# Gate projections in the context steps of two scans: four of 32 moved from the last output steps

## The reference

```python
def token_mixers(h, conv_fn, init_states, with_output, w_in, ...):
    (q_m, k_m, v_m, o_m, gate_m, q_g, k_g, v_g, r_g, lr_g, mg_m, mg_g) = jnp.split(h @ w_in, cuts, axis=-1)
    ...
    hm_f, st_mf = mlstm_scan(qm, km, vm, gm[0, 0], gm[0, 1], st_mf, with_output)
    hm_b, st_mb = mlstm_scan(flip_t(qm), flip_t(km), flip_t(vm), flip_t(gm[1, 0]), flip_t(gm[1, 1]), st_mb, with_output)
    ...
    og_f, st_gf = gla_scan(qg, kg, vg, split_heads(log_a[0], GLA_HEADS), st_gf, with_output)
    og_b, st_gb = gla_scan(flip_t(qg), flip_t(kg), flip_t(vg), flip_t(split_heads(log_a[1], GLA_HEADS)), st_gb, with_output)
    ...
    y_m = merge_heads_rms(hm_f + flip_t(hm_b), ml_norm, h.dtype) * jax.nn.sigmoid(o_m)
    y_g = merge_heads_rms(og_f + flip_t(og_b), gla_norm, h.dtype) * jax.nn.silu(r_g)
    y = jax.nn.sigmoid(mg_m) * (y_m @ w_proj_m) + jax.nn.sigmoid(mg_g) * (y_g @ w_proj_g)
```

## Time and profile before

| what | value |
|---|---|
| median of 3 runs | 2488.88 us (2486.9 to 2498.27) |
| profiled execution | 2488.79 us |
| its span, first to last instruction | 2487.1 us |
| TensorE, VectorE, ScalarE, GpSimd busy | 87%, 57%, 41%, 34% of the span |
| mean granted TensorE clock | 0.935 |
| mLSTM scan, first to last matmul | 641.2 to 955.0 us |
| GLA scan, first to last matmul | 961.5 to 1427 us |

### The profile page before, as it was taken

The page is one execution under the profiler, slowest core; times in us unless marked ns, Lnnn a source line. Parts: engine busy times, 40 slices in busy tenths (PEclk is TensorE's granted clock), DMA queues, the critical chain, the costliest instruction groups (busy, mean ns, idle before and its releaser), DMA issues. The chain is left out here.

```text
span 2487.1 us, 26742 instructions
## 1 busy us (share of the span) xinstructions
PE 2170.5 (87%) x10286; PEld 1756.2 (71%) x10286; DVE 1421.4 (57%) x1711; ACT 1009.6 (41%) x1263; POOL 846.4 (34%) x630
## 2 busy tenths in 40 slices
PE   6979979995599995799999959999759899999992
PEld 1268868884487884688888737788557778887882
DVE  0536542102433332788988535444258899998993
ACT  1422210111144443355455444432216676766762
POOL 5300000100255664366766511220112344443441
PEclk9989999997799997899999969999859999999996
DMA  7733324212354665233345376573348966459535
GB/s 275 247 75 97 98 85 170 80 51 109 120 181 150 177 182 179 80 128 119 115 124 136 77 227 208 159 228 115 106 185 342 360 223 192 118 178 344 154 60 161
DMA packets 262890, 398.75 MB, mean 160 GB/s; under 512 B 27046, under 2 KB 186918, under 8 KB 255980
## 3 DMA queue, kind: packets, MB, share of 16 engines
q1 hardware_dynamic: 233068, 243.90, 30.9%
q0 software_dynamic: 27968, 147.89, 19.0%
q10 hardware_dynamic: 1728, 5.25, 0.6%
HBM read 401.68 MB, written 88.67 MB: 197 GB/s over the span
## 5 line engine op out<-in xcount | busy, mean ns | idle before, releaser
L2584 DVE TENSOR_TENSOR ex_w_lo<-ex_raw,ex_w_hi 128x2048 fp32r<-128x2048 f32 x186 | 415.9, 2283 | 40.4 <-ACT ex_w_hi L2446 40.4
L2446 ACT ACTIVATE ex_w_hi<-ex_raw 128x2048 fp32r<-128x2048 f32 x182 | 337.8, 1909 | 177.6 <-DMA ex_raw<-in_w_up_dram,rt_w_rows 99.6
L682 POOL DMA_DIRECT2D vals<-rows_stage x40 | 21.8, 545 | 438.5 <-ACT rows_stage L674 438.5
L2316 POOL DMA_INDIRECT ex_raw<-in_w_up_dram,rt_w_rows x60 | 73.7, 1229 | 147.5 <-DVE ex_w_lo L2584 142.3
L2009 DVE TENSOR_TENSOR mo_w_lo<-mo_w,mo_w_hi 128x1024 fp32r<-128x1024 f32 x48 | 59.8, 1245 | 102.6 <-ACT mo_w_hi L1906 102.5
L1544 PEld LDWEIGHTS gl_lv_ps<-gl_q_level,gl_k_level 128*128 128x128 f32 x896 | 108.1, 194 | 11.0 <-issue 8.2
L2316 POOL DMA_INDIRECT ex_raw<-in_w_down_dram,rt_w_rows x30 | 52.4, 1748 | 183.2 <-DVE ex_w_lo L2584 183.2
L1544 PE MATMUL gl_lv_ps<-gl_q_level,gl_k_level 128*128 128x64 f32 x896 | 110.5, 276 | 3.3 <-DVE gl_scores L1674 1.7
L908 PE MATMUL gl_u_ps<-half_hi,gl_u_w_hi 128*128 128x512 f32 x256 | 108.0, 422 | 4.6 <-ACT gl_u_exp L926 4.6
L908 PE MATMUL ml_u_ps<-half_hi,ml_u_w_hi 128*128 128x512 f32 x256 | 105.4, 412 | 7.2 <-ACT ml_u_exp L926 7.2
L2120 PE MATMUL mo_ps<-mo_branch_hi,mo_w_hi 128*128 128x512 f32 x256 | 105.5, 412 | 6.9 <-DVE mo_w_lo L2009 6.4
(11 more groups left out here) (401 smaller groups left out, 6058.9 us busy)
## 6 DMA issues: line engine op xcount, KB each, us to landing
fr_w<-in_w_mod_dram SPq DMA_DIRECT2D x12, 2048.0 KB, 10.4
ml_u_w<-in_w_in_dram SPq DMA_DIRECT2D x32, 512.0 KB
gl_u_w<-in_w_in_dram SPq DMA_DIRECT2D x32, 512.0 KB, 5.0
vals<-rows_stage POOLq DMA_DIRECT2D x40, 256.0 KB, 2.3
ml_v<-vals SPq DMA_DIRECT2D x20, 512.0 KB, 3.9
gl_v<-vals SPq DMA_DIRECT2D x20, 512.0 KB, 3.4
qk_w<-in_w_in_dram SPq DMA_DIRECT2D x16, 512.0 KB, 4.8
rows_w<-in_w_in_dram SPq DMA_DIRECT2D x8, 1024.0 KB, 7.1
```

The lines of the kernel that those rows point to most:

```text
L2316: pool.indirect_dma_start(out=raw[:, q, :], out_offset=None, in_=sources[q], in_offset=bass.IndirectOffsetOnAxis(ap=w_rows[:, q, b:b + 1], ...
L2446: act.activation(hi[:, q, h], raw[:, q, h], ACT.Copy).then_inc(hi_done[q], 1)
L2584: dve.tensor_tensor(lo[:, q, at], raw[:, q, at], hi[:, q, at].bitcast(F32), ALU.subtract)\
```

## The change

The 32 units of each scan are given out in another way. Units 0 to 3 stand in the context steps 0 to 3, one each, behind the state products. Output steps 4 to 15 have two units each as before (`unit_in(u)` = 2n + 4 and `unit_after(u)` = 2n + 5), and output steps 16 to 19 have one each, units 28 to 31, in the first of the two places. In the mLSTM scan the transposes of the keys for steps 1 to 4 now stand ahead of the unit of the step before. The loads, the weight copies, the subtractions, `take`, `plus_one`, `finish` and the stores are given out in step with it on SyncE, ScalarE and GpSimd. The wait for the GLA scan's half of the tokens goes with its first unit to step 0. No instruction is added or removed in count.

```diff
@@ -853,6 +853,25 @@
     return 2 * i + 1 - u % 2
 
 
+ONE_UNIT = FIRST_OUT
+
+
+def unit_in(u):
+
+    n = u - FIRST_OUT
+    if n < 0:
+        return None
+    return FIRST_OUT + 2 * n - max(0, n - (OUTS - ONE_UNIT))
+
+
+def unit_after(u):
+
+    n = u - FIRST_OUT
+    if n < 0:
+        return u if u >= 0 else None
+    return unit_in(u) + 1 if n < OUTS - ONE_UNIT else None
+
+
 class GateUnits:
...
@@ -1030,22 +1049,21 @@
             load_rows(FIRST_OUT + 1)
             for u in range(STEPS):
                 n = u - FIRST_OUT
-                if n >= 0:
-                    units.load(sp, 2 * n + 2)
-                    units.load(sp, 2 * n + 3)
-                if n >= 1:
-                    units.store(sp, 2 * n - 2)
+                for g in (unit_in(u), unit_after(u)):
+                    if g is not None:
+                        units.load(sp, g + 2)
+                if unit_in(u - 1) is not None:
+                    units.store(sp, unit_in(u - 1))
                 if FIRST_OUT + 2 <= u + 2 < STEPS:
                     load_rows(u + 2)
-                if u + 2 < STEPS and n < 0:
+                if n < 0:
                     load_v(u + 2)
-                if n >= 1:
-                    units.store(sp, 2 * n - 1)
+                if unit_after(u - 1) is not None:
+                    units.store(sp, unit_after(u - 1))
                 if n >= 0 and first_visit(u):
                     store_h(u)
-                if u + 2 < STEPS and n >= 0:
+                if n >= 0 and u + 2 < STEPS:
                     load_v(u + 2)
-            units.store(sp, UNITS - 2)
             units.store(sp, UNITS - 1)
             units.all_stored(sp)
             for d in range(2):
@@ -1170,16 +1184,19 @@
                 n = u - FIRST_OUT
                 if n >= 0:
                     products(u)
-                if kept(u):
+                if kept(u) and not 0 < u <= FIRST_OUT:
                     keys(u)
                 if n >= 0:
-                    units.multiply(pe, 2 * n)
+                    units.multiply(pe, unit_in(u))
                     outputs(u)
                 if kept(u):
                     state(u, 0)
-                if n >= 0:
-                    units.multiply(pe, 2 * n + 1)
-                if kept(u):
+                if n < 0:
+                    state(u, 1)
+                    keys(u + 1)
+                if unit_after(u) is not None:
+                    units.multiply(pe, unit_after(u))
+                if kept(u) and n >= 0:
                     state(u, 1)
 
         @block.vector
...
@@ -1408,23 +1427,21 @@
             units.low(pool, 0)
             units.low(pool, 1)
             for u in range(STEPS):
-                n = u - FIRST_OUT
+                n, g, late = u - FIRST_OUT, unit_in(u), unit_after(u - 1)
                 if n >= 0:
                     inter(u)
-                if n >= 1:
-                    units.plus_one(pool, 2 * n - 1)
-                    units.scale(pool, 2 * n - 2)
-                    units.low(pool, 2 * n + 1)
-                    if not first_visit(u - 1):
-                        add_o(u - 1)
+                if late is not None:
+                    units.plus_one(pool, late)
+                    units.scale(pool, late - 1)
+                    units.low(pool, late + 2)
+                if n >= 1 and not first_visit(u - 1):
+                    add_o(u - 1)
                 if FIRST_OUT <= u + 1 < STEPS:
                     lower_levels(u + 1)
-                if n >= 0:
-                    units.plus_one(pool, 2 * n)
-                    if n >= 1:
-                        units.scale(pool, 2 * n - 1)
-                    units.low(pool, 2 * n + 2)
-            units.plus_one(pool, UNITS - 1)
+                if g is not None:
+                    units.plus_one(pool, g)
+                    units.scale(pool, g - 1)
+                    units.low(pool, g + 2)
             add_o(STEPS - 1)
 
         @block.scalar
@@ -1480,27 +1497,29 @@
             units.high(act, 0)
             units.high(act, 1)
             for u in range(STEPS):
-                n = u - FIRST_OUT
+                n, g, late = u - FIRST_OUT, unit_in(u), unit_after(u - 1)
+                if n >= 0 and late is not None:
+                    units.take(act, late)
                 if n >= 1:
-                    units.take(act, 2 * n - 1)
                     leave(u - 1)
                 if kept(u):
                     keys_out(u)
-                if n >= 1:
-                    units.high(act, 2 * n + 1)
-                    units.finish(act, 2 * n - 2)
+                if n >= 0 and late is not None:
+                    units.high(act, late + 2)
+                    units.finish(act, late - 1)
                 if u + 1 < STEPS:
                     logs(u + 1)
-                if n >= 0:
-                    units.take(act, 2 * n)
-                    units.high(act, 2 * n + 2)
-                if n >= 1:
-                    units.finish(act, 2 * n - 1)
+                if n < 0 and late is not None:
+                    units.take(act, late)
+                    units.high(act, late + 2)
+                    units.finish(act, late - 1)
+                if g is not None:
+                    units.take(act, g)
+                    units.high(act, g + 2)
+                    units.finish(act, g - 1)
                 if u + 1 < STEPS:
                     factors(u + 1)
-            units.take(act, UNITS - 1)
             leave(STEPS - 1)
@@ -1576,25 +1595,29 @@
                 if n < 0:
                     decays(u + 1)
                     state_sum(u)
+                    if u == 0:
+                        pe.wait_ge(half_loaded, 32)
+                    units.multiply(pe, unit_after(u))
                 else:
+                    g, late = unit_in(u), unit_after(u)
                     level(u, 0)
                     if u + 1 < STEPS:
                         decays(u + 1)
                     level(u, 1)
                     diagonal(u)
-                    if n == 0:
-                        pe.wait_ge(half_loaded, 32)
-                    units.multiply(pe, 2 * n, range(KD // 2))
+                    units.multiply(pe, g, range(KD // 2))
                     level(u, 2)
                     level(u, 3)
-                    units.multiply(pe, 2 * n, range(KD // 2, KD))
+                    units.multiply(pe, g, range(KD // 2, KD))
                     if kept(u):
                         state_sum(u)
-                    units.multiply(pe, 2 * n + 1, range(KD // 2))
+                    if late is not None:
+                        units.multiply(pe, late, range(KD // 2))
                     level(u, 4)
                     level(u, 5)
                     level(u, 6)
-                    units.multiply(pe, 2 * n + 1, range(KD // 2, KD))
+                    if late is not None:
+                        units.multiply(pe, late, range(KD // 2, KD))
                     outputs(u)
 
         @block.vector
```

77 lines of the change are left out of this document (37 added, 40 removed).

## The result

The changed kernel takes **2495.02 us** (median of 20 runs, 2490.37 to 2504.84); the kernel before, on the same chip, 2489.12 us (20 runs, 2484.57 to 2498.27). The ratio is 1.0019, with an interval of 1.0011 to 1.0028: the change costs some 5 us (5.9 us between the medians). The interval tells this small loss apart from nothing; it lies inside the 0.5% that count as no change and inside the range of 2479 to 2500. The profiled execution has a span of 2492.7 us and a mean clock of 0.934.

A forecast was written before the change was run, and what follows sets the result against it. TensorE was taken to bound output steps, VectorE close behind in GLA, with TensorE mostly idle in context. Terms +2.4, +11.1 and -13.3 gave +0.2 us on 2488.79: forecast 2489 us, range 2480 to 2498, widened to 2479 to 2500.

The forecast's parts named there:

- (b): GLA context: units 1 to 3 wait for ScalarE's copy of the unit before, behind the logarithms; +1.9 us twice.
- (d): GLA step 4: TensorE idles less before it, so part of the low clock there may go; -1.3 us.
- (a): GLA context start: the first unit waits for the low half of the tokens and starts at low clock; +7.8 us.
- mLSTM, forecast +2.4: mLSTM scan: context 17.4 us longer, last four output steps -15.0 us together; 2.4 us slower.
- (c): GLA context up to step 4: last unit covered, but GpSimd's lower levels queue behind an addition and a subtraction; +0.8 us.
- GLA, last four steps, forecast -13.3: GLA output steps 16 to 19 and stage end: -13.3 us, not -22.6, with VectorE's work as the floor.
- the half unit (2.8 us) only covers part of this wait: Late GLA output steps: half of the second unit covers only part of TensorE's wait for VectorE's masks.
- the stop of 2.2 us: GLA step 17: VectorE's stop goes with its weight subtraction, but a copy and later subtraction hit key factors; -2.3 us.
- Rival 1: Both scans: idle time takes units free and each one removed at the end is paid back; 2461 us, chance 5%.
- Rival 2: GLA context: the clock stays at the low level throughout; +22 us, 2511 us, chance 13% with half-way forms.
- Rival 3: Context: order on ScalarE and SyncE makes a queue the limit; +5 to +10 us, 2496 us, chance 8%.

The follow-up runs named there:

- ml_only: The change in the mLSTM scan alone, with the GLA scan of the kernel before; 2493.04 us, ratio 1.0018.
- gl_no_half: The GLA change alone, without loading the scan's half of the tokens and without TensorE's wait for it; 2491.27 us (one run).
- gl_late3: The GLA change alone, but three units moved, into context steps 1 to 3, none in step 0; 2488.9 us, ratio 1.0004.
- experiment 8: The GLA change alone, with GpSimd making step 4's lower levels ahead of its unit work in the last context step; 2493.18 us (one run).
- gl_best: gl_late3 plus unread matmuls: 12 ahead of the levels in steps 17 and 18, 22 in context step 3; 2484.09 us, ratio 0.9975.
- b_step4: The kernel before, with 34 unread matmuls added in the third GLA context step, ahead of step 4; 2485.82 us, ratio 0.9985.
- gl_best2: gl_best with GpSimd's lower levels for step 4 first and 14 instead of 22 unread matmuls there; 2488.63 us, ratio 0.9981.
- gl_fill: The GLA change alone, with 12 unread matmuls ahead of the last levels in steps 16, 17 and 18; 2486.83 us, ratio 0.9982.
- experiment 5: The GLA change alone, with ScalarE's copy of the unit ahead of turned keys and logarithms in context steps; 2489.74 us (one run).
- gl_fill2: The GLA change alone, with 12 unread matmuls ahead of the last levels in steps 16 and 18 only; 2486.35 us, ratio 0.9993.

## Why the prediction was right, and where it was not

The forecast was "no change", and the result is no change by its own bound. The number itself was some 6 us low, as much as the whole effect, and a bound of 12.4 us forgives that. There is luck in it too: in the GLA context the term (b) was too high by 1.4 us, which hides most of the 1.8 by which (d) was too low, and at the end one step came out shorter than forecast while two came out longer. The mechanisms of (a) and of the mLSTM scan were right; the price of the uncovered waits was not.

**mLSTM, forecast +2.4.** The context was to take 32.8 us and took 33.21; the last four steps were to be 13.4, 13.4, 12.4 and 19.0 and were 13.41, 13.41, 12.36 and 19.24. The terms measured give +17.8 - 14.8 = +3.0, and +1.6 in the total, with 1.7 us less in steps 4 to 15, which is spread. This part of the prediction is right step by step, with the chains that it named: in steps 16 and 17 the second states wait 1.06 us for VectorE's update, in the last step the products wait 2.27 us for ScalarE's copy. Only the 2.27 us wait in front of the last products was a risk that it did not price: 1.65 us in ml_only.

**GLA (a), forecast +7.8.** Measured +8.4 (21.29 against 12.86). The low half came 13.4 us after the first transposes, where I had 13.0, and the unit took 7.89 where I had 7.6. Right, as is the reason: gl_no_half and gl_late3 take the wait away and the time with it.

**GLA (b), forecast +1.9 twice.** Measured +1.2 twice. The waits for ScalarE's copy are there (1.56 us). The term is mis-sized in the way from the transposes to the unit: I took 5.9 us, which is 6.2 less 0.3 for a faster clock, and it was 5.29 (994.09 to 999.38). The transposes and decays run at the full clock now (0.60 and 0.66 us for 1.12 and 1.11), which is worth about 0.9.

**GLA (c), forecast +0.8.** Measured +1.1. The queue on GpSimd is +2.1 of it (experiment 8); the other -0.9 is put down to the clock, which no run separates.

**GLA (d), forecast -1.3.** Measured **+0.5, the wrong sign**. I reasoned that TensorE idles less before step 4. It does, but the idle time that was left, 5.66 us, is enough for the clock to fall (mean 0.84 in step 4, 0.86 before). Filling that wait was worth 3.7 us where the clock then held (gl_best) and nothing where it fell in the next waits (b_step4, gl_best2). So what counted were the waits beside the stretch and not the share of idle time in the stretch before it.

**GLA, last four steps, forecast -13.3.** Measured -9.9, on the stretches of rows 1 and after: step 16 +1.0 for -1.7, step 17 -3.75 for -2.3, step 18 -0.65 for -3.2, step 19 -5.4 for -5.4, the end -1.1 for -0.7. The step that failed is the sentence "the half unit (2.8 us) only covers part of this wait". It is true for the time that it covers; I let the wait of some 2.9 us appear and did not ask what it does to the clock. In gl_fill, where only this is repaired, steps 16 and 18 are 23.76 and 20.93 us by these stretches, and the prediction had 23.6 and about 20.9. So the chain through VectorE was sized rightly there, and the low clock was the missing term: 2.5 us in step 16 and 2.5 in step 18. Step 17 went the other way. VectorE's masks end 17.85 us into it in place of 20.12, so the stop of 2.2 us went whole, and the copy and the later subtraction that I set against it cost nothing; the step is 21.53 us, not 23.

**The rivals.** Rival 1, idle time is free, is false at both ends: steps 16 to 18 fell by 3.4 us together, though three units of 5.66 us are gone from them. Rival 2 put the low clock in the wrong place: it did not stay low in the context (mean 0.84 there, against 0.64 before), since the pauses of 1.56 us did not lower it; it came at the other end. Rival 3, a queue as the limit: ScalarE's order alone is not (experiment 5), and GpSimd's cost 2.1 us in one step (experiment 8).

## What to carry to other kernels

When a change takes work off TensorE, look at what wait its absence uncovers, and price the matmuls behind that wait at the lower clock as well: here 12 or 22 matmuls without use, put ahead of three such waits, took the change with three units from a ratio of 1.0004 to 0.9975. They do not hold the clock each time. Work moved into "idle" context steps must have all its inputs there; the first of the four units met a transfer that had been hidden by 35 us of slack. And before moving an instruction of GpSimd off the critical queue, see which VectorE instruction it will lie beside then.

## What the runs showed of the chip that I had not expected

- Waits of 2.27 to 2.9 us were enough to lower the granted clock while the next matmuls ran, but not each time: after the same 2.27 us the products took 1.16 us in one kernel and 2.08 in the other. Waits of 1.08 and 1.11 us behind fillers lowered it in step 18 of gl_fill2 and in step 17 of gl_best2, and 1.09 and 1.11 us in the same steps of gl_fill and gl_best did not. Waits of 0.85 and 1.09 us close together lowered it in b_step4, where 0.69 and 1.10 us in gl_best did not. Steps 16 and 18 with one unit and no filler came out between 26.2 and 27.8 us and between 22.9 and 24.6 us in different kernels with the same code there. What tells these apart stays open.
- The Trainium skill (TensorE: Matmul & The Clock Gate, "Loop structure matters more than you think") asks for loops in which matmuls stay back to back, with a wait for a DMA as the case that lets the clock fall. No row here shows that case, since the clock was at 0.50 already ahead of the two waits for a DMA in the context (8.82 and 3.62 us). What the trace adds is that a wait of 2.9 us for VectorE does it too, in the midst of a step in which TensorE is busy for 22.42 of 26.24 us.
- A busy TensorE did not bring the clock back at once: at the start of step 4 of the kernel before it is busy all through 1020 to 1026 us, with matmuls of 64 to 128 columns, and the granted clock stays at 0.50.
